# The forget floor ahead of the query copy on ScalarE, and the exponents of the head two on at the end of the step on VectorE

## The chip, the cores and the metric

The kernel runs on one core of one Trainium2 chip. The metric is the device time of one execution in microseconds; the median of several runs stands for a kernel. Five engines work in the core, each through its own list of instructions in order, and they wait for each other on semaphores: TensorE (PE: matmuls; PEld: its weight loads), VectorE (DVE), ScalarE (ACT), GpSimd (POOL) and SyncE (SP), which issues most of the transfers.

## What is computed

Two blocks of a model, one after the other, on 512 tokens of width 1024 in float32. The first block has a layer with attention and a layer with a gated recurrence; the second has a long convolution, windowed attention, pooling and a mixture of 16 experts. The change lies in the recurrence, of which this is what matters:

```python
def hgrn2_mixer(u, w_in, lb, out_gain, w_out):
    proj = u @ w_in
    q, fl, inp, g = jnp.split(proj, ...)
    log_f = jnp.logaddexp(jnp.log(lbf), jnp.log1p(-lbf) + jax.nn.log_sigmoid(fl))
    k = -jnp.expm1(log_f)
    def step(state, xs):                      # per chunk of tokens, 8 heads
        qb, kb, gb, ib = xs
        b = jnp.cumsum(gb, axis=-2)
        diff = b[..., :, None, :] - b[..., None, :, :]
        decay = jnp.exp(jnp.where(causal[:, :, None], diff, -jnp.inf))
        scores = jnp.einsum('bhtd,bhsd,bhtsd->bhts', qb, kb, decay)
        o = scores @ ib + jnp.einsum('bhtd,bhdv->bhtv', qb * jnp.exp(b), state)
        b_last = b[..., -1:, :]
        state = jnp.exp(b_last[..., 0, :])[..., None] * state + \
            jnp.einsum('bhsd,bhsv->bhdv', kb * jnp.exp(b_last - b), ib)
        return state, o
    _, o = lax.scan(step, state0, (qc, kc, gc, ic))
    o = o * lax.rsqrt(jnp.mean(o * o, axis=-1, keepdims=True) + EPS) * out_gain
    return (o * jax.nn.silu(gh)).reshape(B, S, REC_VWIDTH) @ w_out
```

## The kernel before

Each engine's list is written out by hand, and nothing reorders it. The recurrence goes head by head, h = 0 to 7, on tiles of 128 channels by 512 tokens; a head's 512 tokens are four chunks of 128. The decays between two tokens are split over seven levels (block sizes 1 to 64): for a level the exponents are differences to the middle of each block, so that they never overflow. One step h does this:

- TensorE (loop at L972): "diag" (L977), seven "level" jobs (L987), "kw" (L993, transposes of kd1), "t1" of head h - 1 (L966), the q projection of head h + 2 (L827), the three "state" jobs (L1011), the output "o1" (L1015 and L1019), and the forget projection of head h + 3 (L827). In heads 6 and 7 a small matmul for the filter of the second block stands there too (L1001, L1005), and gate projections take the place of the q and forget projections.
- VectorE (loop at L2000): forget_in(h + 2) (L1852, L1854), exponents(h + 1) (L1881 and L1882, 14 subtractions of 128 x 256), head_scores(h) (L1898 for "diag", then seven predicated copies L1910), head_turned(h - 1) (L1946), forget_log(h + 2) (L1859, L1861, L1862), head_states(h) (L1918, L1921), chunk_exponents(h + 1) (L1890), head_mean_square(h) (L1926), forget_sum(h + 2) (L1867 and the scan L1868), head_normed(h) (L1932 to L1940).
- ScalarE (loop at L1510): level_exps(h + 1) (L1473, one instruction over 3584 columns), the copy of "kw" (L1370), forget_softplus(h + 2) (L1457, L1459), the query copy of head h + 2 (L1370), forget_floor(h + 2) (L1464 to L1469), head_squares(h) (L1492), chunk_exps(h + 1) (L1480 to L1484).
- GpSimd (loop at L733): decayed_levels(h + 1), 14 products (L721, L723), after the level exponentials of h + 1 and once TensorE has read level 6 of head h; the power for the root (L738) after the mean square; decayed_chunk(h + 1), two products (L728, L729).

What ties them: forget_log waits for the softplus, the floor for forget_log, forget_sum for the floor, the exponents for the sum of their head; the mean square waits for the squares, the squares for "o1". The exponents of a head are kept in one of two buffers and may be written once TensorE has read level 6 of the head two before.

The results of TensorE go to eight PSUM banks, which a ledger (class Ledger) gives to the jobs in turn. A job that reuses a bank waits until the reader of the job eight before has emptied it. A step has 16 jobs: "diag", seven levels, "kw", "t1", the q projection, three states, "o1", the forget projection. So "kw" waits for the reader of "diag" of the same step (L1898), level 5 for the reader of "o1" of the step before (L1937), and level 6 for the reader of the forget projection before it (L1852).

Of the kernel before, what the change touches and what calls it, by code (L numbers as in the profile page):

```python
# [29 lines left out]
RH = 8  # L30
# [107 lines left out]
def before_state(h):  # L138

    return [("q1", h + 2)] if h + 2 < RH else [("g1", 3 if h == RH - 2 else 5)]  # L140


def after_output(h):

    if h + 3 < RH:
        return [("f1", h + 3)]
    return {RH - 3: [("g1", 2)], RH - 2: [("g1", 4)], RH - 1: [("g1", 6), ("g1", 7)]}[h]
# [163 lines left out]
def two_blocks(nc, a, out):  # L311

    ctx = ExitStack()
    with ctx:
# [1026 lines left out]
        def _(act):  # L1341
# [25 lines left out]
            def copy(dst, name, src=None, scale=1.0, func=ACT.Identity):  # L1367
                act.wait_ge(filled, nth(name))
                bank = led.bank(name)
                act.activation(dst, bank[:, :] if src is None else src(bank), func, scale=scale).then_inc(by_act, 1)  # L1370
# [83 lines left out]
            def forget_softplus(h):  # L1454
                w = fwork[h % 2]
                act.wait_ge(f_dve, 4 * h + 1)
                act.activation(w[1], w[1], ACT.Exp).then_inc(f_act, 1)  # L1457
                act.wait_ge(f_act, 6 * h + 1)
                act.activation(w[1], w[1], ACT.Ln, bias=1.0).then_inc(f_act, 1)  # L1459

            def forget_floor(h):
                w = fwork[h % 2]
                act.wait_ge(f_dve, 4 * h + 3)
                act.activation(w[4], w[2], ACT.Abs, bias=lw[0][:, h:h + 1]).then_inc(f_act, 1)  # L1464
                act.activation(k1[h % 2], w[3], ACT.Exp, bias=lw[3][:, h:h + 1]).then_inc(f_act, 1)
                act.wait_ge(f_act, 6 * h + 3)
                act.activation(w[4], w[4], ACT.Exp, scale=-1.0).then_inc(f_act, 1)
                act.wait_ge(f_act, 6 * h + 5)
                act.activation(w[4], w[4], ACT.Ln, bias=1.0).then_inc(f_act, 1)  # L1469

            def level_exps(h):
                act.wait_ge(expo_in, h + 1)
                act.activation(expo[h % 2], expo[h % 2], ACT.Exp).then_inc(expo_done, 1)  # L1473
# [21 lines left out]
            def late_gate(h):  # L1495
                if h >= 3:
                    act.wait_ge(head_gated, h - 2)
                copy(gate1, ("g1", h), func=ACT.Silu)
# [11 lines left out]
            for h in range(RH):  # L1510
                if h + 1 < RH:
                    level_exps(h + 1)
                copy(kw1[:, :, :], ("kw", h), src=lambda b: b[:, 0:384].rearrange("p (c t) -> p c t", c=3))
                if h + 2 < RH:
                    forget_softplus(h + 2)
                else:
                    act.wait_ge(sin_in, h - RH + 3)
                    act.activation((sine_1, sine_2)[h - RH + 2], sine_x, ACT.Sin).then_inc(sin_out, 1)
                for tag, j in before_state(h):
                    if tag == "q1":  # L1520
                        copy(q1[j % 2], ("q1", j))
                    else:
                        late_gate(j)
                if h + 2 < RH:
                    forget_floor(h + 2)
                head_squares(h)
                if h + 1 < RH:
                    chunk_exps(h + 1)
                for tag, j in after_output(h):
                    if tag == "g1":  # L1530
                        late_gate(j)
# [96 lines left out]
        def _(dve):  # L1628
# [177 lines left out]
            for m in range(KT + 1):  # L1806
                if m >= 1:
                    for n in range(2):
                        h = 2 * m - 2 + n
# [13 lines left out]
                if m < KT:  # L1823
                    for n in range(2):
                        h = 2 * m + n
# [38 lines left out]
            def forget_sum(h):  # L1864
                w = fwork[h % 2]
                dve.wait_ge(f_act, 6 * h + 6)
                step(dve.tensor_tensor(w[5], w[5], w[4], ALU.add))  # L1867
                dve.tensor_tensor_scan(b1[h % 2], reset, w[5], 0.0, ALU.mult, ALU.add).then_inc(f_dve, 1)  # L1868
                dve.wait_ge(f_dve, 4 * h + 4)

            def exponents(h):

                e = expo[h % 2]
                if h >= 2:
                    dve.wait_ge(filled, nth(("level", h - 2, LEVELS - 1)))
                for level in range(LEVELS):
                    half = 1 << level
                    ev = e[:, level, :].rearrange("p (n g s) -> p n g s", g=2, s=half)
                    bv = b1[h % 2].rearrange("p (n g s) -> p n g s", g=2, s=half)
                    mid = bv[:, :, 0, half - 1:half].broadcast_to([P, T // (2 * half), half])  # L1880
                    dve.tensor_tensor(ev[:, :, 1, :], bv[:, :, 1, :], mid, ALU.subtract)  # L1881
                    ins = dve.tensor_tensor(ev[:, :, 0, :], mid, bv[:, :, 0, :], ALU.subtract)  # L1882
                ins.then_inc(expo_in, 1)
# [40 lines left out]
            def head_mean_square(h):  # L1924
                dve.wait_ge(o_sq, h + 1)
                dve.tensor_scalar(mean[:, 0:4], ss[:, 0:4], 1.0 / P, EPS, ALU.mult, ALU.add).then_inc(head_mean, 1)  # L1926
                dve.wait_ge(head_mean, h + 1)
# [23 lines left out]
            def late_gate(h):  # L1951
                dst = mixT[1][:, h, :]
                dve.wait_ge(*drained(("t1", h)))
                dve.wait_ge(*drained(("g1", h)))
                dve.tensor_tensor(dst, dst, gate1, ALU.mult).then_inc(head_gated, 1)
# [44 lines left out]
            for h in range(RH):  # L2000
                if h + 2 < RH:
                    forget_in(h + 2)
                if h + 1 < RH:
                    exponents(h + 1)
                head_scores(h)
                if h >= 1:
                    head_turned(h - 1, mixT[1][:, h - 1, :] if h <= 2 else None)
                if h == RH - 2:
                    sine_argument(("fh1",), 0)
                elif h == RH - 1:  # L2010
                    sine_argument(("fh2",), 1)
                    sum_filter_weights()
                if h + 2 < RH:
                    forget_log(h + 2)
                head_states(h)
                if h + 1 < RH:
                    chunk_exponents(h + 1)
                if h == RH - 2:
                    late_gate(3)
                head_mean_square(h)  # L2020
                if h + 2 < RH:
                    forget_sum(h + 2)
                elif h == RH - 1:
                    late_gate(5)
                head_normed(h)
                for tag, j in after_output(h):
                    if tag == "g1" and j < RH - 1:
                        late_gate(j)
# [73 lines left out]
            for m in range(1, NH // 2 + 1):  # L2102
                for n in range(2):
                    h = 2 * m - 2 + n
# [208 lines left out]
```

## Time and profile before

| | |
|---|---|
| median of 3 runs | 2184.64 us (2183.11 to 2184.93) |
| profiled execution | 2189.95 us, its span 2188.2 us |
| busy: PE, PEld, DVE, ACT, POOL | 2043.8, 981.8, 597.4, 421.5, 198.5 us |
| mean granted clock of TensorE | 0.967 of full speed |
| recurrence | from about 515 to 795 us of the span |

The rows further down come from four views. The waits name, for an instruction that found its engine idle, who released it. The timeline gives instructions of one engine in order of time, merged where a line repeats, and in brackets the idle time just before. A view of stretches gives the busy time of every engine in a given piece of the span and PEclk, the clock granted to TensorE as a share of 2.4 GHz (0.50 is 1.2 GHz). The view of one line or tensor gives the spread of durations. Times count from the start of the span.

### The profile page before, as it was taken

How to read it: one execution, taken by the hardware profiler on the slowest of the kernel's cores; microseconds unless marked ns; L12 is line 12 of the kernel's file. 1: busy time of each engine (PE TensorE's matmuls, PEld its weight loads, DVE VectorE, ACT ScalarE, POOL GpSimd, SP SyncE). 2: the span in 40 equal slices, each digit the busy share in tenths (PEclk: the TensorE clock that was granted, in tenths of full speed). 3: DMA queues.
4: the chain of work that ended last, by engine and by line, in shares of the span. 5: the costliest groups of instructions: out<-in, count | busy, mean ns of one | idle time of the engine just before them, and what ended most of it. 6: DMA issues, size and time to landing. Idle time of an engine off the chain costs nothing.

```text
span 2188.2 us, 20253 instructions
## 1 busy us (share of the span) xinstructions
PE 2043.8 (93%) x8224; PEld 981.8 (45%) x8224; DVE 597.4 (27%) x1316; ACT 421.5 (19%) x818; POOL 198.5 (9%) x260
## 2 busy tenths in 40 slices
PE   8999999999988999999999698999989898989896
PEld 3455454444565554454655443434343332434333
DVE  2233342312677632314443410101010101101012
ACT  1233331114554511110230000000101010000002
POOL 3100000001545500000110000000000000000000
PEclk9999999999999899999999799999999999999998
DMA  7211012202111141240240599999999999999995
GB/s 262 80 58 58 1 56 89 77 10 77 39 39 39 43 183 36 75 141 0 77 156 37 211 413 429 427 428 427 428 428 427 428 428 427 428 428 427 428 427 220
DMA packets 87644, 486.36 MB, mean 222 GB/s; under 512 B 5663, under 2 KB 37754, under 8 KB 63488
## 3 DMA queue, kind: packets, MB, share of 16 engines
q1 hardware_dynamic: 84896, 480.79, 54.1%
q0 software_dynamic: 2368, 4.16, 0.7%
q8 instruction: 66, 1.08, 0.2%
q14 instruction: 26, 0.21, 0.0%
q10 hardware_dynamic: 288, 0.11, 0.0%
HBM read 482.90 MB, written 2.34 MB: 222 GB/s over the span
## 4 chain that ended last, share of the span: by engine, by line
PE 80%; DMA 12%; DVE 5%; ACT 2%; issue 1%; POOL 0%; POOLq 0%; ACTq 0%; DVEq 0%
PE bank L827 19%; PE bank L835 17%; PE bank L1284 13%; DMA arena<-in_w_up 12%; PE bank L1315 10%; PE bank L1235 3%; PE bank L1153 3%; PE bank L1261 2%; PE bank L907 2%; PE bank L1305 1%; PE bank L1039 1%; PE bank L817 1%; PE bank L1108 1%; PE bank L925 1%; PE bank L915 1%
## 5 line engine op out<-in xcount | busy, mean ns | idle before, releaser
L1284 PE MATMUL bank<-arena 128*64 128x512 f32 x2048 | 467.7, 615 | 69.8 <-DMA arena<-in_w_up 69.8
L827 PE MATMUL bank<-arena 128*128 128x512 f32 x1024 | 457.2, 606 | 0.0
L835 PE MATMUL bank<-arena 128*128 128x512 f32 x832 | 363.0, 596 | 5.1 <-issue 4.3
L1284 PEld LDWEIGHTS bank<-arena 128*64 128x64 f32 x2048 | 160.9, 142 | 373.7 <-issue 373.5
L827 PEld LDWEIGHTS bank<-arena 128*128 128x128 f32 x1024 | 196.9, 195 | 245.1 <-issue 244.7
L835 PEld LDWEIGHTS bank<-arena 128*128 128x128 f32 x832 | 157.9, 191 | 199.6 <-issue 198.4
L1315 PE MATMUL bank<-arena 128*64 128x512 f32 x960 | 217.2, 612 | 0.0
L1370 ACT ACTIVATE arena<-bank 128x512 f32<-128x512 f32 (+3 forms) x140 | 76.5, 551 | 536.8 <-PE bank L835 197.4
L2228 DVE TENSOR_TENSOR arena<-arena,bank 128x512 f32<-128x512 f32 x64 | 42.0, 685 | 410.5 <-PE bank L1261 409.8
L1587 ACT ACTIVATE arena<-bank 64x512 f32<-64x512 f32 x64 | 37.7, 589 | 553.3 <-PE bank L1284 510.9
L2243 DVE TENSOR_TENSOR arena<-bank,arena 64x512 f32<-64x512 f32 x64 | 44.4, 695 | 362.6 <-ACT arena L1587 360.7
L1315 PEld LDWEIGHTS bank<-arena 128*64 128x64 f32 x960 | 69.4, 141 | 135.7 <-issue 134.6
L801 POOL TENSOR_TENSOR small<-small 128x4 f32<-128x4 f32 x1 | 1.0, 1013 | 964.4 <-DVE small L2260 964.4
L1235 PEld LDWEIGHTS bank<-arena 128*128 128x128 f32 x512 | 62.8, 201 | 7.8 <-issue 7.8
L1235 PE MATMUL bank<-arena 128*128 128x128 f32 x512 | 64.5, 288 | 1.2 <-DVE arena L2200 1.2
L1604 ACT ACTIVATE arena<-bank,small 64x512 f32<-64x512 f32 x30 | 20.5, 682 | 211.1 <-PE bank L1315 210.9
L1153 PE MATMUL bank<-arena 128*128 128x512 f32 x128 | 58.3, 610 | 1.6 <-DVE arena L2134 1.6
L1261 PE MATMUL bank<-arena 128*128 128x512 f32 x128 | 57.3, 599 | 2.2 <-ACT arena L1612 2.2
L721 POOL TENSOR_TENSOR arena<-arena 128x256 f32<-128x256 f32 x56 | 48.2, 860 | 97.6 <-ACT arena L1473 84.9
L1389 ACT ACTIVATE arena<-arena,small 128x128 f32<-128x128 f32 (+3 forms) x96 | 49.9, 521 | 24.1 <-DVE small L1703 23.4
L987 PE MATMUL bank<-arena 128*128 128x64 f32 x448 | 50.9, 274 | 0.0
L987 PEld LDWEIGHTS bank<-arena 128*128 128x128 f32 x448 | 50.7, 192 | 0.0
(289 smaller groups left out, 1598.9 us busy)
## 6 DMA issues: line engine op xcount, KB each, us to landing
arena<-in_w_gate SPq DMA_DIRECT2D x64, 2048.0 KB, 24.6
arena<-in_w_up SPq DMA_DIRECT2D x64, 2048.0 KB, 28.5
arena<-in_w_down SPq DMA_DIRECT2D x60, 2048.0 KB, 23.9
arena<-in_att_w_in SPq DMA_DIRECT2D x12, 1024.0 KB, 11.3
arena<-in_rec_w_in SPq DMA_DIRECT2D x12, 1024.0 KB, 5.8
arena<-in_ple_w_gate SPq DMA_DIRECT2D x4, 2048.0 KB, 14.4
arena<-in_w_down SPq DMA_DIRECT2D x8, 1024.0 KB, 18.1
arena<-in_w_in SPq DMA_DIRECT2D x6, 1024.0 KB, 7.8
```

The lines of the kernel that those rows point to most:

```text
L721: pool.tensor_tensor(ev[:, :, 1, :], ev[:, :, 1, :], qv[:, :, 1, :], ALU.mult).then_inc(decayed, 1)
L827: mm = pe.matmul(bank[:, :], w[:, k, c:c + P], xT[:, k, :], start=(k == 0), stop=(k == KT - 1))
L835: mm = pe.matmul(bank[:, 0:n], xT[:, k, P * i:P * i + P], w[:, k, c:c + n], start=(k == 0), stop=(k == kt - 1))
L987: mm = pe.matmul(bank[:, 64 * c:64 * c + 64], kl1[:, level, P * c:P * c + P], ev[:, n * c:n * c + n, 1, :], start=True, stop=True)
L1153: mm = pe.matmul(bank[:, :], mixT2[:, k, P * i:P * i + P], w[:, k, :], start=(k == ks[0]), stop=(k == ks[-1]))
L1235: mm = pe.matmul(bank[:, P * k:P * k + P], hn[:, i, 256 * kq + odd:256 * kq + 256:2], ohp[:, i, :], start=(i == 0), stop=(i == TT - 1))
L1261: pe.matmul(bank[:, :], ohT[:, P * i:P * i + P], yrow[:, 512 * half:512 * half + 512], start=True, stop=True).then_inc(moe_filled, 1)
L1284: mm = pe.matmul(banks[f][64 * part:64 * part + 64, :], xe[:, k, CAP * (e % 2):CAP * (e % 2) + CAP], w[:, kk, 512 * f:512 * f + 512], star ...
L1315: mm = pe.matmul(bank[64 * half:64 * half + 64, :], hT[:, 4 * b + j, :], wd[:, j, 512 * half:512 * half + 512], start=(b == 0 and j == 0), ...
L1370: act.activation(dst, bank[:, :] if src is None else src(bank), func, scale=scale).then_inc(by_act, 1)
L1389: act.activation(s, s, ACT.Exp, bias=nmx[:, r:r + 1], accum_out=rs[:, r:r + 1]).then_inc(probs_in, 1)
L2243: dve.tensor_tensor(hrow[64:P, f, :], banks[f][64:P, :], sil[f % 2][64:P, :], ALU.mult).then_inc(h_ready2, 1)
```

## The change

On ScalarE, forget_floor(h + 2) goes ahead of the copy that follows the q projection. On VectorE, exponents(1) stays at the start of step 0; the exponents of every later head are written at the end of the step two before it, behind the mean square and ahead of head_normed. For that forget_sum(h + 2) goes ahead of head_mean_square(h).

```diff
@@ scalar, for h in range(RH) @@
                     act.activation((sine_1, sine_2)[h - RH + 2], sine_x, ACT.Sin).then_inc(sin_out, 1)
+                if h + 2 < RH:
+                    forget_floor(h + 2)
                 for tag, j in before_state(h):
                     if tag == "q1":
                         copy(q1[j % 2], ("q1", j))
                     else:
                         late_gate(j)
-                if h + 2 < RH:
-                    forget_floor(h + 2)
                 head_squares(h)
@@ vector, for h in range(RH) @@
                 if h + 2 < RH:
                     forget_in(h + 2)
-                if h + 1 < RH:
-                    exponents(h + 1)
+                if h == 0:
+                    exponents(1)
                 head_scores(h)
@@ vector, the end of the same loop @@
                 if h == RH - 2:
                     late_gate(3)
+                if h + 2 < RH:
+                    forget_sum(h + 2)
                 head_mean_square(h)
                 if h + 2 < RH:
-                    forget_sum(h + 2)
+                    exponents(h + 2)
                 elif h == RH - 1:
                     late_gate(5)
                 head_normed(h)
```

VectorE at the end of a step, first piece: from forget_sum (L1867, L1868) on; the lines with a minus are head_normed and, of the next step, forget_in.

```order
 L1867 TENSOR_TENSOR arena<-arena 128x512
 L1868 SCALAR_TENSOR_TENSOR arena<-tab,arena 128x512
-L1932 TENSOR_TENSOR small<-small 128x4
-L1933 TENSOR_TENSOR small<-small 128x4
-L1934 TENSOR_SCALAR small<-small 128x4
-L1935 TENSOR_TENSOR small<-small 128x4
-L1937 TENSOR_TENSOR arena<-bank,small 128x512
-L1940 COPY small<-small 128x1
-L1852 COPY arena<-bank 128x512
-L1854 SCALAR_TENSOR_TENSOR arena<-arena 128x512
+L1926 TENSOR_SCALAR small<-small 128x4
 L1881 TENSOR_TENSOR arena<-arena 128x256
```

The mean square L1926 now follows the sum, and the exponents (L1881, L1882, fourteen in all) follow it directly.

Second piece, 14 exponents further on, up to L1898, the first instruction of head_scores:

```order
 L1882 TENSOR_TENSOR arena<-arena 128x4x64
+L1932 TENSOR_TENSOR small<-small 128x4
+L1933 TENSOR_TENSOR small<-small 128x4
+L1934 TENSOR_SCALAR small<-small 128x4
+L1935 TENSOR_TENSOR small<-small 128x4
+L1937 TENSOR_TENSOR arena<-bank,small 128x512
+L1940 COPY small<-small 128x1
+L1852 COPY arena<-bank 128x512
+L1854 SCALAR_TENSOR_TENSOR arena<-arena 128x512
 L1898 TENSOR_TENSOR arena<-bank,tab 128x512
```

head_normed and forget_in stand behind the exponents now, directly ahead of L1898.

ScalarE in step 0, before: the end of the softplus (L1459), the query copy (L1370), the floor (L1464 to L1469), the squares (L1492).

```order
L1459 ACTIVATE arena<-arena 128x512
L1370 ACTIVATE arena<-bank 128x512
L1464 ACTIVATE arena<-arena,small 128x512
L1465 ACT_TABLE_LOAD
L1465 ACTIVATE arena<-arena,small 128x512
L1467 ACTIVATE arena<-arena 128x512
L1469 ACT_TABLE_LOAD
L1469 ACTIVATE arena<-arena 128x512
L1492 ACTIVATE arena,small<-bank 128x128 x4
```

The same place with the change:

```order
L1459 ACTIVATE arena<-arena 128x512
L1464 ACTIVATE arena<-arena,small 128x512
L1465 ACT_TABLE_LOAD
L1465 ACTIVATE arena<-arena,small 128x512
L1467 ACTIVATE arena<-arena 128x512
L1469 ACT_TABLE_LOAD
L1469 ACTIVATE arena<-arena 128x512
L1370 ACTIVATE arena<-bank 128x512
L1492 ACTIVATE arena,small<-bank 128x128 x4
```

The query copy moved from ahead of the floor to between the floor and the squares.

## Rows read from the trace of the kernel before

**Rows 1.** TensorE's waits, whole kernel: line, releaser, total us, times, longest.
```profile
PE bank L993 <- DVE arena L1898: 18.0, 6, 3.1
```

**Rows 2.** Stretches: busy us of PE, PEld, DVE, ACT, POOL, then PEclk, DMA, GB/s.
```profile
560.00:580.00 20.00, 20.00 (x112) 14.21 (x111) 9.56 (x15) 13.64 (x15) 11.48 (x14) 1.00 0.00 1
595.00:596.00 1.00, 1.00 (x3) 0.50 (x2) 0.93 (x3) 1.00 (x2) 0.00 (x0) 0.50 0.00 0
880.00:900.00 20.00, 19.16 (x57) 9.04 (x56) 10.09 (x24) 2.83 (x5) 0.54 (x1) 1.00 0.25 78
```

**Rows 3.** TensorE's timeline: start, duration, line, operation, [idle before]; three places.
```profile
574.09 0.83 PE L1011 MATMUL bank<-arena 128*128 128x128 f32 x6
...
576.32 7.03 PE L827 MATMUL bank<-arena 128*128 128x512 f32 x16
583.19 1.05 PE L977 MATMUL bank<-arena 128*128 128x128 f32 x8
...
593.56 0.52 PE L993 MATMUL bank<-tab,arena 128*128 128x128 f32 x3 [3.11 <-DVE arena L1898]
...
595.18 8.38 PE L827 MATMUL bank<-arena 128*128 128x512 f32 x16
...
753.13 0.83 PE L1011 MATMUL bank<-arena 128*128 128x128 f32 x6
...
769.32 0.50 PE L993 MATMUL bank<-tab,arena 128*128 128x128 f32 x3
...
770.19 1.07 PE L1005 MATMUL bank<-arena,fw 64*64 64x512 f32 x2
```

**Rows 4.** Timeline of VectorE: end of step h = 2 and the next.
```profile
640.36 0.17 DVE L1926 TENSOR_SCALAR small<-small 128x4 f32<-128x4 f32 x1 [4.68 <-ACT arena L1492]
640.57 0.69 DVE L1867 TENSOR_TENSOR arena<-arena 128x512 f32<-128x512 f32 x1
641.29 1.23 DVE L1868 TENSOR_TENSOR_SCAN arena<-tab,arena 128x512 f32<-128x512 f32 x1
...
642.95 1.27 DVE L1934 TENSOR_SCALAR small<-small 128x4 f32<-128x4 f32 x1
644.25 0.91 DVE L1935 TENSOR_TENSOR small<-small 128x4 f32<-128x4 f32 x1
...
647.33 0.42 DVE L1881 TENSOR_TENSOR arena<-arena 128x256 f32<-128x256 f32 x1
...
652.03 0.68 DVE L1898 TENSOR_TENSOR arena<-bank,tab 128x512 f32<-128x512 f32 x1
652.75 3.90 DVE L1910 COPY_PREDICATED arena<-maskt,bank 128x256 f32<-128x256 int32 x7
656.55 0.74 DVE L1946 TENSOR_SCALAR arena<-bank,cols 128x512 f32<-128x512 f32 x1
...
659.30 1.10 DVE L1861 TENSOR_TENSOR arena<-arena 128x512 f32<-128x512 f32 x1
```

**Rows 5.** Timeline of ScalarE, h = 3: query copy, first of floor, first square.
```profile
662.26 0.60 ACT L1370 ACTIVATE arena<-bank 128x512 f32<-128x512 f32 x1 [4.08 <-PE bank L827]
662.75 0.71 ACT L1464 ACTIVATE arena<-arena,small 128x512 f32<-128x512 f32 x1
...
667.87 0.26 ACT L1492 ACTIVATE arena<-bank 128x128 f32<-128x128 f32 x1
```

**Rows 6.** GpSimd: three rows of its timeline; durations ns (min/median/max) of L721.
```profile
640.68 1.45 POOL L738 TENSOR_TENSOR small<-small 128x4 f32<-128x4 f32 x1 [3.72 <-DVE small L1926]
642.93 1.27 POOL L728 TENSOR_TENSOR arena<-arena 128x512 f32<-128x512 f32 x1 [0.80 <-ACT arena L1484]
644.15 0.99 POOL L729 TENSOR_TENSOR arena<-arena 128x384 f32<-128x384 f32 x1
...
L721 POOL TENSOR_TENSOR arena<-arena x56: 714/838/1183, 539.9 to 753.4; 128x256 f32<-128x256 f32 x56
```

**Rows 7.** Issues of the experts' gate weights: durations, first and last start.
```profile
L630 SPq DMA_DIRECT2D arena<-in_w_gate x64: 327/328/581, 1114.7 to 2112.2; - x64
```

## The prediction

> **What bounds the kernel now.** I read the waits of TensorE first, then the granted clock in short windows, then the timelines of the four compute engines through one step of the recurrence. In the recurrence TensorE is busy but for 18.0 us, in six pieces of up to 3.1 us, at L993 on VectorE's L1898 [rows 1]. L993 is the transposes of kd1 (job "kw") in heads 1 to 6. The ledger gives jobs eight banks in turn, and a head has 16 jobs, so "kw" of a head takes the bank of "diag" of the same head, which L1898 (first instruction of head_scores) empties. L1898 comes late because the 14 subtractions of exponents(h + 1) stand ahead of it in VectorE's order: 647.33 to 652.03, L1898 directly behind at 652.03 [rows 4].
>
> The idle time is not its whole price. A stretch of one microsecond after such a gap shows a granted clock of 0.50 (1.2 GHz), while the step in which TensorE never waits shows 1.00 [rows 2]. The projection after the gap then takes 8.38 us where the same 16 matmuls took 7.03 [rows 3].
>
> **A period without the wait.** I measure a period from the start of the state matmuls (L1011) to the next. The six from 574.09 to 753.13 (heads 1 to 6) take 179.04, 29.84 on average [rows 3]. At full clock and with no wait a period would be:
> - 574.09 to the moment at which "kw" could have started, 593.56 less its idle 3.11 = 590.45: 16.36 us;
> - "kw" and the transposes of "t1": 769.32 to 770.19 in head 7, where nothing waits: 0.87;
> - the q projection, as long as the forget projection with its 16 matmuls, 576.32 to 583.19: 6.87.
> Together 24.10 us. Inside it, counted from its start: forget projection at 2.2, "diag" at 9.1, seven level groups of 0.91 (an eighth of 583.19 to 590.45) from 10.0, so level 5 at 14.6 and level 6 at 15.5, "kw" at 16.4. The sixth period has one filter matmul more (1.07) [rows 3].
>
> **The change on ScalarE.** The forget floor (L1464 to L1469, 662.75 to 667.87 = 5.12 us) now goes ahead of the query copy, which waited for the q projection until 662.26. Its input is L1861, done at 660.40 [rows 4, 5]. So the floor starts some 2.3 us earlier. Behind it now wait the query copy (0.49 until L1464) and the squares of o1. The copy's readers are far: GpSimd multiplies with that query a head later, and its bank is wanted by level 1 at 10.9 of the period, the copy ending near 3.6. The squares end near 4.7 instead of 6.9. Nothing is added here, so the cost is nothing, as long as the floor ends before about 10 of the period.
>
> **The change on VectorE.** The same instructions run; the sum of forget h + 2 goes ahead of the mean square, and 14 subtractions (4.70 us) move from in front of L1898 of the next head to in front of head_normed of this one. Moving them alone would leave L1898 where it was, since both places lie ahead of it; the gain is that VectorE is not idle before them (L1926, the mean square, let it stand 4.68 us for the squares, with the sum queued behind it [rows 4]) and that TensorE no longer runs slow. What is late next? I follow the loop through VectorE and ScalarE that no longer passes through TensorE:
> - floor 5.12 [rows 5];
> - sum, 640.57 to 642.52: 1.95 [rows 4]; mean square 0.17, say 0.2 [rows 4];
> - exponents 4.70 [rows 4];
> - what GpSimd takes from VectorE. L1934 and L1935, four columns each, took 1.27 and 0.91 beside L728 and L729 of 1.27 and 0.99 at the same moments [rows 4, 6]. Without company such an instruction takes 0.17 (L1926), so these two multiplications cost VectorE 1.10 + 0.75 = 1.85. They will now meet the exponents, which also read two SBUF operands: I charge 1.85 there;
> - head_normed and forget_in: 642.52 to 647.33 less that same 1.85: 2.96 [rows 4];
> - L1898 0.72, the seven predicated copies to 656.55 3.80, L1946 0.65, the two steps of forget_log 2.2 (L1861 1.10) [rows 4].
> Sum 24.15, with three handovers between the engines of some 0.05 each (an estimate) 24.3 us. TensorE's own period is 24.10. So the two are nearly equal, and VectorE's loop sets the pace by a little. In the period the exponents then run from about 5.3 to 11.9, L1937 is done by 13.4 (its bank is wanted by level 5 at 14.6), L1852 by 14.2 (level 6 at 15.5), L1898 by 15.5 ("kw" at 16.4). Three waits that could take the place of the old one each have about 1 us to spare. ScalarE's level exponentials and GpSimd's level products come earlier too; GpSimd starts once level 6 has been read, 16.4, and needs 14 products of 0.84 in the median, 11.7 us [rows 6], until 3.8 of the next period, ahead of "diag" at 9.1.
>
> The bounds of the contention: below, none (VectorE in the shadow of TensorE, 24.10). Above, the exponents lose all the time of the three GpSimd operations beside them, 1.45 for the power and 2.26 for the two products, 3.7 [rows 6]: the loop is then 26.15. I take 1.85, the row of the same two GpSimd operations.
>
> Here a rule of the Trainium skill speaks against the change ("SBUF — State Buffer", the summary of rules for kernel authors): a VectorE instruction with two SBUF inputs and a GpSimd instruction that reads SBUF shut each other out, and the second to issue waits for the whole of the first. This trace agrees: L1861 took 1.10 beside a product of GpSimd where L1867, equally large, took 0.69 alone [rows 4]. By that rule taken for every exponent the loss would be that of the rival on the slower side, below.
>
> **The sum.** Six periods of 24.3 and the filter matmul's 1.07: 146.9, against 179.04: 32.1 us less. Of this about 18 is the idle time of [rows 1] and 14 the time lost at 1.2 GHz and while it is regained. Behind the recurrence everything hangs on TensorE's progress: the first expert slab is issued at 1114.7 behind a TensorE job, and the stream of slabs then runs without a break [rows 7]. So I pass all of it on, less 0.1 for small waits in heads 6 and 7: 32.0. The profiled execution, 2189.95 us with a span of 2188.2, would become 2158 with a span of 2156. The median of the runs is 2184.64, 5.3 below the profiled one; less 32.0 it is 2152.6.
>
> **Rivals.**
> 1. *A new, shorter wait.* If GpSimd costs the exponents more than 2.8 (1.85 and the spare microsecond), level 5 waits for L1937. At the bound of 3.7 a period is 26.2, the six with the filter matmul 158.3: 20.7 less, 2163.9. Between: 2156 to 2164. For it speaks that all three margins are near 1 us; against it that no row shows more than 1.85 lost to these operations. Chance 0.25.
> 2. *The clock does not come back.* The level groups are short matmuls, and if these keep the clock low, only the 18.0 of idle time goes: 2166.6. Against it: head 0, with the same groups and no gap, ran at 1.00, and so did a stretch with 0.84 us of idle time [rows 2]. Chance 0.04.
> 3. *The gain is lost behind the recurrence,* or TensorE waits as before since something else was late together with L1898: no change. Nothing in the waits shows a second releaser there. Chance 0.04.
> 4. *Slower.* Each of the 14 exponents is shut out by GpSimd, as L1861 was: 14 x 0.41 = 5.7 in place of 1.85. Then the loop is 28.2, TensorE stands about 4 us at level 5, and it comes out of the gap at 1.2 GHz for the levels, "kw" and the projection; with the 2.6 us that a period loses to that now, near 30.8 against 29.84: 6 us slower, 2190. It decides when the exponents take over 10 us instead of 4.7. Against it: GpSimd has only 3.7 us of work there. Chance 0.03.
>
> **The numbers.** My case, a period of 24.1 to 24.6 (2151 to 2155), has 0.64; the likeliest time is 2152.6. The range 2149 to 2165 takes in no contention at all (33.4 less: 2151), a little for the clock elsewhere, and the whole of rival 1. What a measurement can tell from no change is about 0.2% (4.4 us). Faster by more than that: cases 0, 1 and 2, 0.93. Within: rival 3, 0.04. Slower: rival 4, 0.03.
>
> **What would show it.** Right: L993's wait on L1898 gone or below 0.5 us, granted clock 1.00 from 560 to 750, periods of 24.1 to 24.6 us, L1934 and L1935 at 0.17, the exponents at 6 to 7 us for 14 with L728 and L729 beside them, the floor starting within 0.1 us of L1861's end. Wrong: a wait of TensorE at L987 on L1937 (rival 1; over 2 us rival 4), clock below 1.00 without gaps (rival 2), a saved recurrence but the first expert slab not 32 us earlier (rival 3).

## The result, and the profile after

| | before | changed |
|---|---|---|
| median (runs) | 2184.25 us (4) | 2153.68 us (4), 2150.02 to 2158.01 |
| ratio | | 0.9861, 95% interval 0.9842 to 0.9880 |
| profiled execution, its span | 2189.95, 2188.2 us | 2150.02, 2148.2 us |
| six periods of the recurrence, heads 1 to 6 | 179.04 us | 148.40 us |

The change is worth 30.6 us; 32.0 had been forecast (2152.6, counted from a median of 2184.64). A second set of runs gave 2153.00 beside 2184.18, ratio 0.9845 (0.9829 to 0.9861).

The 18.0 us of [rows 1] are gone. These are the waits of TensorE in the changed kernel from 540 to 780 us (line, releaser, us in total, times, longest): the one at L993 is down to 0.2 us, once.

```profile
PE bank L966 <- DVE arena L1910: 0.7, 3, 0.3
PE bank L827 <- DVE arena L1910: 0.7, 4, 0.2
PE bank L987 <- DVE arena L1937: 0.3, 1, 0.3
PE bank L993 <- DVE arena L1898: 0.2, 1, 0.2
```

The timeline of TensorE, for comparison with [rows 3]: the first two periods, 567.74 to 593.29 and to 617.39, and the end of the sixth. In the first, small waits at four places; in the second, none from "kw" (609.48) to the next period, and the projection behind it takes 7.11 us where 8.38 stood.

```profile
567.74 0.83 PE L1011 MATMUL bank<-arena 128*128 128x128 f32 x6
...
582.62 1.97 PE L987 MATMUL bank<-arena 128*128 128x64 f32 x16 [0.32 <-DVE arena L1937]
584.75 0.52 PE L993 MATMUL bank<-tab,arena 128*128 128x128 f32 x3 [0.16 <-DVE arena L1898]
585.55 0.63 PE L966 MATMUL bank<-tab,arena 128*128 128x128 f32 x4 [0.28 <-DVE arena L1910]
586.35 7.10 PE L827 MATMUL bank<-arena 128*128 128x512 f32 x16 [0.17 <-DVE arena L1910]
593.29 0.83 PE L1011 MATMUL bank<-arena 128*128 128x128 f32 x6
...
609.48 0.50 PE L993 MATMUL bank<-tab,arena 128*128 128x128 f32 x3
...
610.44 7.11 PE L827 MATMUL bank<-arena 128*128 128x512 f32 x16
617.39 0.83 PE L1011 MATMUL bank<-arena 128*128 128x128 f32 x6
...
716.14 0.83 PE L1011 MATMUL bank<-arena 128*128 128x128 f32 x6
```

A stretch of the changed kernel, as in [rows 2]. TensorE is busy in nearly all of 600 to 620, at a granted clock of 1.00 (2.4 GHz); the whole stretch from 560 to 750 shows 1.00 too.

```profile
600.00:620.00 20.00, 19.97 (x114) 14.31 (x114) 17.71 (x34) 10.88 (x11) 12.66 (x15) 1.00 0.00 1
```

VectorE at the end of step 0, the place of [rows 4] one period after the other: the mean square, then the fourteen exponents, two of them at 1.48 and 1.21 us where the others take 0.41, then head_normed with L1934 at 0.17 instead of 1.27, and L1898.

```profile
574.21 0.17 DVE L1926 TENSOR_SCALAR small<-small 128x4 f32<-128x4 f32 x1
574.42 0.43 DVE L1881 TENSOR_TENSOR arena<-arena 128x256 f32<-128x256 f32 x1
...
576.11 1.48 DVE L1882 TENSOR_TENSOR arena<-arena 128x256 f32<-128x256 f32 x1
577.51 1.21 DVE L1881 TENSOR_TENSOR arena<-arena 128x256 f32<-128x256 f32 x1
...
581.38 0.17 DVE L1934 TENSOR_SCALAR small<-small 128x4 f32<-128x4 f32 x1
...
581.78 0.69 DVE L1937 TENSOR_TENSOR arena<-bank,small 128x512 f32<-128x512 f32 x1
...
583.92 0.68 DVE L1898 TENSOR_TENSOR arena<-bank,tab 128x512 f32<-128x512 f32 x1
```

What stands beside the two slow ones is on GpSimd, at the same moments:

```profile
575.85 1.46 POOL L728 TENSOR_TENSOR arena<-arena 128x512 f32<-128x512 f32 x1
577.27 1.17 POOL L729 TENSOR_TENSOR arena<-arena 128x384 f32<-128x384 f32 x1
```

And the floor on ScalarE no longer stands behind the query copy as in [rows 5]; it waits for VectorE's L1861, which ended at 591.08:

```profile
591.11 0.72 ACT L1464 ACTIVATE arena<-arena,small 128x512 f32<-128x512 f32 x1 [2.85 <-DVE arena L1861]
```

**The two profiled executions differ by more than the change.** Their spans are 40.0 us apart, the medians 30.6. The first state matmuls already start 6.35 us earlier (574.09 and 567.74), in code that the change does not touch. The stretch from 50 to 150 us shows why, first the kernel before, then the changed one: the granted clock was 0.95 there in one execution and 1.00 in the other.

```profile
50.00:150.00 100.00, 98.25 (x260) 44.50 (x259) 25.70 (x75) 24.42 (x53) 13.02 (x24) 0.95 0.24 75
```

```profile
50.00:150.00 100.00, 98.25 (x281) 45.25 (x280) 26.92 (x77) 24.90 (x55) 11.75 (x22) 1.00 0.25 79
```

In a second profiled execution of the changed kernel the same stretch was at 0.95 and the first state matmuls started at 573.78, yet its six periods took 148.41 us. All twelve profiled executions fall on one side or the other: at 0.95 in this stretch the first state matmuls start at 573.2 to 574.1 (four of them), at 1.00 at 567.1 to 568.4 (eight). So this is chance from one execution to the next. Of the 40.0 us, 6.35 lie ahead of the recurrence, 30.6 in its six periods and some 3 further back. I read the experiments by the sum of the six periods (from the first start of L1011's group to the seventh), with the medians beside it. The two kernels that were profiled twice gave the same sum to 0.01 us; both ran at full clock in every period. The kernel before and the other experiments have one trace each, and where the clock falls in some periods the sum may repeat less well.

### The profile page after: what moved, and what is told of

Same layout as the page of the kernel before. It is cut to its first block, busy times and chain, and to the rows that moved or that the text cites. A ratio compares the mean times of both kernels' runs of the same rounds, so it can differ in the third digit from the quotient of the medians.

```text
span 2148.2 us, 20253 instructions
## 1 busy us (share of the span) xinstructions
PE 2023.5 (94%) x8224; PEld 971.8 (45%) x8224; DVE 598.5 (28%) x1316; ACT 421.7 (20%) x818; POOL 199.3 (9%) x260
## 4 chain that ended last, share of the span: by engine, by line
PE 81%; DMA 12%; DVE 4%; ACT 1%; issue 1%; POOL 0%; POOLq 0%; ACTq 0%; DVEq 0%
PE bank L827 19%; PE bank L835 17%; PE bank L1284 13%; DMA arena<-in_w_up 12%; PE bank L1315 10%; PE bank L1235 3%; PE bank L1153 3%; PE bank L1261 2%; PE bank L907 2%; PE bank L1305 1%; PE bank L987 1%; PE bank L1039 1%; PE bank L817 1%; PE bank L1108 1%; PE bank L925 1%
## 5 line engine op out<-in xcount | busy, mean ns | idle before, releaser
L827 PE MATMUL bank<-arena 128*128 128x512 f32 x1024 | 446.1, 594 | 0.7 <-DVE arena L1910 0.7
L835 PE MATMUL bank<-arena 128*128 128x512 f32 x832 | 362.0, 595 | 5.1 <-issue 4.2
L827 PEld LDWEIGHTS bank<-arena 128*128 128x128 f32 x1024 | 192.4, 190 | 238.0 <-issue 237.9
L835 PEld LDWEIGHTS bank<-arena 128*128 128x128 f32 x832 | 157.6, 191 | 198.9 <-issue 197.7
L1370 ACT ACTIVATE arena<-bank 128x512 f32<-128x512 f32 (+3 forms) x140 | 76.4, 550 | 512.4 <-PE bank L835 196.5
L1235 PEld LDWEIGHTS bank<-arena 128*128 128x128 f32 x512 | 62.3, 200 | 7.8 <-issue 7.8
L1261 PE MATMUL bank<-arena 128*128 128x512 f32 x128 | 57.3, 600 | 2.2 <-ACT arena L1612 2.2
L1153 PE MATMUL bank<-arena 128*128 128x512 f32 x128 | 56.7, 595 | 1.6 <-DVE arena L2136 1.6
L721 POOL TENSOR_TENSOR arena<-arena 128x256 f32<-128x256 f32 x56 | 48.3, 862 | 75.9 <-PE bank L987 51.1
L987 PE MATMUL bank<-arena 128*128 128x64 f32 x448 | 51.1, 274 | 0.3 <-DVE arena L1937 0.3
L987 PEld LDWEIGHTS bank<-arena 128*128 128x128 f32 x448 | 50.7, 192 | 0.4 <-issue 0.4
```

The lines of the kernel that those rows point to most:

```text
L721: pool.tensor_tensor(ev[:, :, 1, :], ev[:, :, 1, :], qv[:, :, 1, :], ALU.mult).then_inc(decayed, 1)
L827: mm = pe.matmul(bank[:, :], w[:, k, c:c + P], xT[:, k, :], start=(k == 0), stop=(k == KT - 1))
L835: mm = pe.matmul(bank[:, 0:n], xT[:, k, P * i:P * i + P], w[:, k, c:c + n], start=(k == 0), stop=(k == kt - 1))
L987: mm = pe.matmul(bank[:, 64 * c:64 * c + 64], kl1[:, level, P * c:P * c + P], ev[:, n * c:n * c + n, 1, :], start=True, stop=True)
L1153: mm = pe.matmul(bank[:, :], mixT2[:, k, P * i:P * i + P], w[:, k, :], start=(k == ks[0]), stop=(k == ks[-1]))
L1235: mm = pe.matmul(bank[:, P * k:P * k + P], hn[:, i, 256 * kq + odd:256 * kq + 256:2], ohp[:, i, :], start=(i == 0), stop=(i == TT - 1))
```

## Experiments

| kernel | six periods, us | one by one | median, us | ratio to before (95%) |
|---|---|---|---|---|
| before | 179.04 | 29.30 30.01 28.66 29.69 30.20 31.18 | 2184.2 to 2185.5 | 1 |
| changed | 148.40 | 25.55 24.10 24.81 24.34 24.58 25.02 | 2153.68 | 0.9861 (0.9842 to 0.9880) |
| changed, again | 148.41 | 25.54 24.11 24.83 24.31 24.59 25.03 | 2153.00 | 0.9845 (0.9829 to 0.9861) |
| ScalarE's edit alone | 161.24 | 27.42 27.07 27.07 25.51 28.54 25.63 | 2167.46 | 0.9913 (0.9897 to 0.9929) |
| VectorE's edit alone | 169.28 | 27.64 27.47 27.42 27.42 27.42 31.91 | 2175.03 | 0.9944 (0.9930 to 0.9959) |
| before, gap filled with 12 matmuls | 175.26 | 29.01 five times, 30.21 | 2185.00 | 0.9986 (0.9973 to 0.9998) |
| before, gap filled with 6 matmuls | 168.03 | 27.96 27.96 27.95 27.97 27.95 28.24 | 2178.03 | 0.9958 (0.9942 to 0.9973) |
| changed, GpSimd's products held back | 145.21 | 24.48 23.83 23.86 24.07 23.83 25.14 | 2152.19 | 0.9840 (0.9820 to 0.9861) |
| the same, again | 145.21 | 24.48 23.83 23.86 24.06 23.83 25.15 | 2154.85 | 0.9848 (0.9828 to 0.9869) |
| changed, four exponents more | 155.50 | 27.45 25.42 25.59 25.58 25.60 25.86 | 2160.72 | 0.9895 (0.9880 to 0.9910) |
| changed, mean square first | 155.65 | 27.05 25.01 25.66 26.99 24.62 26.32 | 2160.49 | 0.9899 (0.9883 to 0.9915) |
| changed, head_normed first | 157.98 | 28.61 24.57 27.19 25.21 26.58 25.82 | 2164.03 | 0.9900 (0.9885 to 0.9916) |

The sixth period of each has the filter matmul.

### Each edit alone

ScalarE's edit alone:

```diff
+                if h + 2 < RH:
+                    forget_floor(h + 2)
                 for tag, j in before_state(h):
...
-                if h + 2 < RH:
-                    forget_floor(h + 2)
```

> The kernel before with the edit on ScalarE alone (the forget floor of head h + 2 ahead of the query copy); VectorE as before. Theory (the loop through VectorE and ScalarE sets the pace, and the exponents stand ahead of L1898): the floor no longer waits for the q projection, so the loop is shorter by about 2 us a head, but the mean square still holds back the sum. TensorE still waits at L993, 0.5 to 2.6 us instead of 3.1, perhaps by turns, and the clock falls less often: 10 to 20 us faster than before (2165 to 2174). Rival (the edit on ScalarE only makes room, the gain is VectorE's): within 4 us of before, L993 still at 3.1 us a head.

It was 18.1 us faster by the medians and 17.8 by the periods. TensorE's waits there, from 540 to 780:

```profile
PE bank L993 <- DVE arena L1898: 6.4, 5, 2.0
```

The gap at L993 fell from 18.0 to 6.4 us without one instruction of VectorE moved. What held L1898 back was the start of the floor as much as the place of the exponents, and the rival falls. The waits are shorter, but the clock still fell behind four of them, the shortest 0.89 us, in head 3:

```profile
640.14 0.52 PE L993 MATMUL bank<-tab,arena 128*128 128x128 f32 x3 [0.89 <-DVE arena L1898]
```

```profile
641.00:642.00 1.00, 1.00 (x5) 0.91 (x6) 0.96 (x2) 1.00 (x1) 0.00 (x0) 0.50 0.00 0
```

VectorE's edit alone:

```diff
-                if h + 1 < RH:
-                    exponents(h + 1)
+                if h == 0:
+                    exponents(1)
...
+                if h + 2 < RH:
+                    forget_sum(h + 2)
                 head_mean_square(h)
                 if h + 2 < RH:
-                    forget_sum(h + 2)
+                    exponents(h + 2)
```

> The kernel before with the edit on VectorE alone (sum ahead of the mean square, exponents of head h + 2 behind it); ScalarE as before. Theory: the floor waits for the q projection again, 2.3 us later, and so do the sum and everything behind it; TensorE waits 1 to 2 us at level 5 on L1937 and under 0.5 us at L993, periods near 26.3 us: 12 to 20 us faster than before (2164 to 2172), less if the clock falls. Rival (the edit on VectorE is the whole gain): 30 us faster, as the two together, 2154.

It was 10.5 us faster by the medians (9.8 by the periods), less than the 12 to 20 expected, and far from the 30 of the rival, which falls. The wait did move to level 5 on L1937, 1.76 us in every head (10.6 in all). The forecast had named the clock ("less if the clock falls") and given it no price; it fell behind the wait in every head: five periods are 27.42 to 27.64 where 26.3 was expected, and the sixth is 31.91. That one, head 6, is the worst: "kw", "t1", the filter matmul (1.97) and the projection, 9.50 us where 7.03 is full speed, all run slow:

```profile
721.75 2.92 PE L987 MATMUL bank<-arena 128*128 128x64 f32 x16 [1.76 <-DVE arena L1937]
724.46 0.85 PE L993 MATMUL bank<-tab,arena 128*128 128x128 f32 x3
...
726.10 1.97 PE L1001 MATMUL bank<-arena,fw 33*64 33x512 f32 x2
727.99 9.50 PE L827 MATMUL bank<-arena 128*128 128x512 f32 x16
```

One-microsecond stretches of the same kernel give the granted clock: 1.00 in the gap, 0.50 in each of those from 723 to 732. (In head 1 it is 0.50 or near it only from 586 to 589.)

```profile
724.00:725.00 1.00, 1.00 (x7) 1.00 (x7) 0.96 (x2) 0.00 (x0) 0.15 (x1) 0.50 0.00 0
...
730.00:731.00 1.00, 1.00 (x3) 0.48 (x2) 0.97 (x2) 0.00 (x0) 1.00 (x2) 0.50 0.00 0
```

The two edits alone give 17.8 and 9.8 us, 27.6 in sum, and together 30.6. TensorE's busy and idle time over the six periods tells where the 3 us are. Idle time goes down by 10.5 and 7.9 us alone and by 16.6 together; busy time, of the same instructions, by 7.3 and 1.9 alone and by 14.0 together. Most of the 3 us is the slow clock, then, which only both edits remove (its granted mean over the six periods is 0.90 before, 0.96 and 0.92 with one edit, 1.00 with both).

### The clock's share

To separate idle time from the slow clock behind it, TensorE was kept at work in the gap of the kernel before, writing columns of the level 6 bank that nobody reads. (The filler is work that the reference does not ask for; nothing of the computation is left out.)

```diff
                 for level in range(LEVELS):
...
+                    if level == LEVELS - 1 and 1 <= h <= RH - 2:
+                        for _ in range(12):
+                            pe.matmul(bank[:, 256:512], ident, i1[:, 0, 0:256], start=True, stop=True)
```

> The kernel before, and in heads 1 to 6 TensorE runs 12 more matmuls of 128x256 ahead of level 6, into columns of its bank that nobody reads. They fill about 2.7 of the 3.1 us in which TensorE was idle; no wait of another engine ends sooner, so the only thing that can change is the clock. Theory (14 of the 32 us are lost to the clock after the gap): granted clock 1.00 through the recurrence, the q projection after the gap at 7.0 instead of 8.4 us, 9 to 15 us faster than before (2169 to 2175). Rival (the time after the gap is not the clock's, or VectorE's loop takes it back since it never waited for TensorE): within 3 us of before.

The six periods are 3.8 us shorter and the median 0.5 (ratio 0.9986), not the 9 to 15 expected; what the clock is worth cannot be read from that, since the filler was too long. The timeline shows 24 instructions and 5.40 us for the 12 matmuls, so that TensorE itself, without a wait and at a clock of 1.00, set a period of 29.01:

```profile
611.46 5.40 PE L988 MATMUL bank<-arena,tab 128*128 128x256 f32 x24
```

With range(6) in place of range(12):

> The kernel before with half the filler: 6 matmuls of 128x256 ahead of level 6 in heads 1 to 6 (the first try with 12 showed 24 instructions and 5.2 us, 2.1 more than the gap, so TensorE itself set a period of 29.01 and the comparison told nothing of the clock's price). Now the filler takes 2.6 of the 3.1 us. Theory: the clock stays at 1.00; the loop before ran from the end of the q projection to L993 (19.47 us) and then through L993, L966 and the next q projection, which are 7.7 us at full clock: a period of 27.2 instead of 29.84, 13 to 16 us faster than before, 2169 to 2172, with a rest of idle time of 0.3 to 0.6 us a head. Rival (what follows the gap is slow for another reason, or the loop does not pass through the projection): periods stay near 29, within 4 us of before.

Periods of 27.96, 11.0 us less over the six, against the 13 to 16 expected; the medians say 6.7, and the interval of the ratio 5.9 to 12.7. Here is one period of it: the filler takes 2.81 us, a rest of 0.52 us remains at L996 (which is L993 shifted by the edit), and the projection behind it is at full speed.

```profile
595.60 0.83 PE L1014 MATMUL bank<-arena 128*128 128x128 f32 x6
...
610.90 2.81 PE L988 MATMUL bank<-arena,tab 128*128 128x256 f32 x12
...
615.07 0.52 PE L996 MATMUL bank<-tab,arena 128*128 128x128 f32 x3 [0.52 <-DVE arena L1901]
615.84 0.63 PE L966 MATMUL bank<-tab,arena 128*128 128x128 f32 x4 [0.26 <-DVE arena L1913]
616.62 7.11 PE L827 MATMUL bank<-arena 128*128 128x512 f32 x16 [0.15 <-DVE arena L1913]
623.56 0.83 PE L1014 MATMUL bank<-arena 128*128 128x128 f32 x6
```

The time from the start of the period to "kw" is 19.47 us, to the hundredth what it was in [rows 3] (574.09 to 593.56): no other engine was late or early by itself. The rest is 8.49 us where I had expected 7.7. Of this "t1" and the projection wait 0.26 and 0.15 us for the predicated copies that follow L1898; their starts are some 0.3 us later still, in the same places, and the view does not show that as idle time. That the time came down at all needs the loop to pass through TensorE: in the kernel before, the floor waited for the copy of the projection, so a faster projection made every later step earlier.

The 11.0 us are what the clock gives back while VectorE's and ScalarE's orders stay as they were. They are not yet its share of the 30.6. For that, here are the six periods of the kernel before, the changed one and the half-filled one; behind the length of the stretch stands TensorE's busy time:

```profile
574.09:753.13 179.04, 160.56 (x742) 104.13 (x740) 128.68 (x248) 93.25 (x146) 95.07 (x109) 0.90 0.12 37
```

```profile
567.74:716.14 148.40, 146.53 (x741) 97.58 (x740) 129.22 (x248) 92.08 (x144) 94.12 (x107) 1.00 0.14 45
```

```profile
567.64:735.67 168.03, 163.02 (x814) 111.40 (x813) 127.24 (x248) 92.59 (x145) 92.13 (x105) 1.00 0.13 40
```

Before, TensorE was idle for 18.5 us, after the change for 1.9, and the same work took 160.6 and 146.5 us busy. So the 30.6 are 16.6 of idle time and 14.0 of busy time, and the granted clock went from 0.90 to 1.00. Busy time is not the clock's to the last microsecond: the kernel with GpSimd's products held back (below) also ran at 1.00 and has 144.7, so I take the 14.0 to be slow clock within some 2 us (an estimate from these rows). The half-filled kernel agrees: 163.0 less six fillers of 2.81 is 146.2, so there the slow clock is gone as well. About 3 us of it came back as waits, for filler and idle time together are 21.9 us where 18.5 were idle.

### What sets the pace now

> The changed kernel with four of the fourteen exponents of heads 2 to 7 written twice (the same values, after a semaphore of VectorE's own): about 1.4 us more on VectorE between the mean square and head_normed. Theory (VectorE's loop sets the pace now, by a little): periods longer by 1.2 to 1.4 us, waits of TensorE at level 5 of about 1 us, 7 to 9 us slower than the changed kernel, 2161 to 2163, if the clock holds. Rival (TensorE sets the pace and VectorE has a microsecond to spare): at most 3 us slower.

```diff
-                for level in range(LEVELS):
+                levels = list(range(LEVELS)) + ([LEVELS - 2, LEVELS - 1] if h >= 2 else [])
+                for at, level in enumerate(levels):
+                    if at == LEVELS:
+                        step(ins)
```

The periods grew by 7.1 us, the median by 7.0 (2160.7, just under the 2161 to 2163 expected). VectorE had nothing to spare: 1.4 us more a head cost 1.2. The first period alone grew by 1.9: its wait at level 5 was 1.8 us, and the clock fell to 0.50 behind it. In the others that wait was 0.2 to 0.4 us, less than the 1 us expected, and the clock stayed at 1.00 from 589 on. TensorE's waits, from 540 to 780, stand where the forecast put the next late thing, at level 5 on head_normed (L1940 here is L1937 shifted), and the copies and L1898 behind it follow:

```profile
PE bank L987 <- DVE arena L1940: 3.5, 6, 1.8
PE bank L966 <- DVE arena L1913: 1.1, 4, 0.3
PE bank L993 <- DVE arena L1901: 0.6, 4, 0.2
```

The other side, GpSimd's two products moved away from the exponents:

```diff
+                if h + 3 < RH:
+                    pool.wait_ge(f_dve, 4 * h + 13)
                 if h + 1 < RH:
                     decayed_chunk(h + 1)
```

> The changed kernel, with one wait more on GpSimd: its two products L728 and L729 begin only when VectorE has finished forget_in of head h + 3 (heads 0 to 4), so that they stand beside L1898 and the predicated copies, which read PSUM, and not beside the exponents. Theory (the two products take 1.85 us from the exponents, and VectorE's loop is just above TensorE's 24.1): all 14 exponents at 0.42, none at 1.2 to 1.5, VectorE 1.8 us a head earlier at L1898, TensorE without any wait in heads 1 to 6, periods 24.1; 1 to 3 us faster than the changed kernel (2151 to 2153), hardly more than the measurement tells. Rival (the slow exponents are slow by themselves, by their strides): the two slow ones stay, periods as in the changed kernel.

Its GpSimd waits for VectorE's L1856 (L1854 shifted, the end of forget_in), and VectorE's exponents of that head, 598.32 to 603.02, ran at 0.41 to 0.43 each, none slower; the pair that was slow in the changed kernel is regular here, so the strides are not the cause.

```profile
606.17 1.27 POOL L728 TENSOR_TENSOR arena<-arena 128x512 f32<-128x512 f32 x1 [6.55 <-DVE arena L1856]
```

```profile
598.32 0.43 DVE L1883 TENSOR_TENSOR arena<-arena 128x256 f32<-128x256 f32 x1
...
603.02 0.15 DVE L1934 TENSOR_TENSOR small<-small 128x4 f32<-128x4 f32 x1
```

TensorE's only wait from 540 to 780 is 0.4 us, in the first head, for the product that is now held back itself:

```profile
PE bank L995 <- POOL arena L729: 0.4, 1, 0.4
```

The periods are 3.2 us shorter in sum, slightly more than the 1 to 3 expected, and the median 1.5. The shortest fall to 23.83, which is then TensorE's own. I had computed 24.10. Both kernels were timed again, side by side:

> The changed kernel once more, beside chunk_late_again on the same chip, since the two were not timed in one call before. Expected 2151 to 2157; the six periods of the recurrence at 148 to 149 us in its profile, as in its first profile (148.4), whatever the rest of the execution does.

> The changed kernel with GpSimd's two products held back until VectorE has finished forget_in. By the six periods of its first profile (145.2 against 148.4) it should be 3 us faster than the changed kernel on the same chip; rival: the 3 us are within what one execution differs from the next, and the medians show nothing.

Both sums came back within a hundredth, 148.41 and 145.21. In the medians, 2153.00 and 2154.85, the 3.2 us are not to be seen: single runs of either kernel lie 7.5 to 8.7 us apart, more than the difference. By the trace this is the best version; by the clock on the wall it cannot be told from the changed kernel.

### The order at the end of the step

```diff
+                head_mean_square(h)
                 if h + 2 < RH:
                     forget_sum(h + 2)
-                head_mean_square(h)
```

> The changed kernel with head_mean_square back ahead of forget_sum; the exponents stay behind both. Theory: the sum then waits for the squares, which end 1.5 us after the floor, so sum and exponents start 1.6 us later in a loop that has nothing to spare: 7 to 10 us slower than the changed kernel, 2161 to 2164. Rival (once the floor is early the order of the two is indifferent): within 2 us of the changed kernel.

7.3 us more in the periods, 6.8 by the medians: the sum must stand ahead of the mean square, since the squares end later than the floor. Of the 7.3, 3.3 are idle time and 3.9 busy time, most of it the clock's (0.98 in the mean). The periods are uneven (27.05, 25.01, ..., 26.99), because the clock fell in some heads and not in others. In head 1 it fell behind a wait of 1.37 us:

```profile
583.28 2.48 PE L987 MATMUL bank<-arena 128*128 128x64 f32 x16 [1.37 <-DVE arena L1937]
```

In head 4 it fell behind waits of 0.44, 0.16 and 0.27 us (L987, L993, L966), and the projection took 8.40 us; one head earlier, waits of 0.45, 0.16 and 0.27 at the same lines left it at 1.00, and the projection took 7.11. The length of the waits alone does not tell whether the clock falls.

```profile
634.42 1.97 PE L987 MATMUL bank<-arena 128*128 128x64 f32 x16 [0.45 <-DVE arena L1937]
...
638.12 7.11 PE L827 MATMUL bank<-arena 128*128 128x512 f32 x16 [0.15 <-DVE arena L1910]
...
660.08 1.97 PE L987 MATMUL bank<-arena 128*128 128x64 f32 x16 [0.44 <-DVE arena L1937]
...
663.83 8.40 PE L827 MATMUL bank<-arena 128*128 128x512 f32 x16
```

And head_normed ahead of the exponents:

```diff
                 head_mean_square(h)
                 if h + 2 < RH:
+                    head_normed(h)
                     exponents(h + 2)
```

> The changed kernel with head_normed ahead of the exponents (after sum and mean square). The bank of o1 is then emptied 5 us earlier, so level 5 has room, but VectorE stands 1.2 to 1.5 us for GpSimd's power in each head. Theory (what counts is VectorE's whole loop, not the one bank): 5 to 9 us slower than the changed kernel, 2159 to 2163, TensorE waiting at L993 on L1898 again, 0.5 to 1.5 us. Rival (the bank of o1 at level 5 is what limits the changed kernel): same or faster than the changed kernel.

9.6 us more in the periods, 10.4 by the medians, slightly past the 5 to 9 expected. VectorE does stand idle for the power as expected, 1.26 us in head 1, but TensorE waits elsewhere: at level 6 on L1852, and at L993 only 0.5 us in all. These waits cost 3.0 us of idle time more than in the changed kernel; the other 6.6 are busy time, mostly because the clock fell to 0.50 in or soon behind each of the three waits at level 6 (1.44, 0.79 and 0.77 us), a price that the forecast did not have.

```profile
PE bank L987 <- DVE arena L1852: 3.0, 3, 1.4
PE bank L993 <- DVE arena L1898: 0.5, 2, 0.3
```

L1852 is the next instruction of VectorE whose bank is wanted once L1937 is early; moving one reader ahead only uncovers the next.

## Why the prediction was right, point by point

- **What bounds.** Right: TensorE, held at L993 by L1898, and slowed behind the gap. The six periods came down by 30.6 us, against 32.1 in the sum. Their mean without the filter matmul is 24.56, inside the 24.1 to 24.6 that was named as the sign, near its upper end.
- **TensorE's own period.** 24.10 was computed, 23.83 is what it takes when nothing waits (kernel with the products held back). Of the 0.27, 0.17 lies in the moment at which "kw" could start: I had taken it as 593.56 less the idle time, 16.36 us into the period; in a head without a wait "kw" starts at 609.48 - 593.29 = 16.19. Idle time counts from the modelled end of the last matmul, and the rows show that the next one starts a little before it. The other 0.10 lies in "kw" and "t1", 0.87 in head 7 and 0.77 where nothing waits. That the second period of the changed kernel is 24.10 to the hundredth is luck: behind "kw" it takes 7.91 us against 7.64 in the kernel with the products held back, though the view shows no wait there. The error did no harm, since VectorE's loop was the longer one.
- **VectorE's loop.** 24.3 was computed; from one L1926 to the next it took 24.13 (574.21 to 598.34), and a mean of 24.4 over the next five. The terms held to within 0.25 us (forget_log took 1.95 here and 2.2 a head later, for 2.2). The floor started 0.03 us behind L1861, the exponents with their contention took 6.57 us (574.42 to 580.99) for 4.70 + 1.85 = 6.55.
- **The contention.** The charge of 1.85 was the least sure term and came out at (1.48 - 0.42) + (1.21 - 0.41) = 1.86. The same two products of GpSimd cost VectorE the same time in both places. The prediction says of L1934 and L1935 that they too read two SBUF operands; L1934 reads one tensor with two constants, and was held up all the same (1.27 for 0.17). Held back behind forget_in, the products cost VectorE nothing: L1898 took 0.68 beside them.
- **The mis-sized term** is the first period: 25.55, where all six had been put at 24.3 (the last with the filter matmul's 1.07 on top). In head 0 forget_log waited 2.80 us for the softplus, the floor ended 4.0 us into the period instead of 3.0, and the sum (L1867) met a product of GpSimd and took 1.15 instead of 0.69. That is 1.25 of the 1.5 us by which the sum was off. The other 0.46 of this kind returns in every second head or so (L1867 at 1.14 in the third), which makes the 24.8 among the 24.1.
- **The split of the gain,** 18 idle and 14 clock, held: 16.6 and 14.0 by TensorE's idle and busy time. With the gap filled and nothing else changed, 11.0 of it reach the period and about 3 turn into waits.
- **That moving the exponents alone leaves L1898 where it was** missed in one point: VectorE's whole edit alone brought 9.8 us, by the sum that no longer waits for the squares. But a wait at level 5, 10.6 us in all, took the place of the 18.0 at L993 (the wait of rival 1), and the clock went on falling behind it, so that busy time came down by only 1.9 of the 14.0 us.
- **Rivals.** Rival 1 appeared as 0.32 us in one head. Rival 2 (the short matmuls of the levels keep the clock low) falls: 1.00 from 560 to 750. Rival 3 falls: the first expert slab is issued 36.9 us earlier (1114.7 and 1077.8), the 6.35 that came ahead of the recurrence and the 30.6 of it. Rival 4's size was 5.7 us of contention a head; 1.86 was there.

## What to carry to other kernels

When an engine waits for another, follow the loop from that release back to itself through all engines before moving anything: here it ran through two queues, in each of which an instruction that nobody needed yet stood ahead of one that the loop waited for, and each of the two orders was worth part of the gain. Price a regular gap on TensorE by the period and not by the idle time, since the matmuls behind it can run slow (nearly half of the 30.6 us here), and look at what is late next before counting on more than the slack of that bank or buffer. And read a difference of a few microseconds from sums over the same stretch of several traces; for the two kernels traced twice here they repeated to 0.01 us where whole executions differed by 8.

## What the runs showed of the hardware

- The granted clock of TensorE fell to 0.50 behind regular gaps much shorter than the 3.1 us of the kernel before: 1.76 us in every head (VectorE's edit alone), 0.89 with 0.26 behind it (ScalarE's edit alone), 0.77 (head_normed first). It stayed at 1.00 behind 0.66 and 0.26 in one head of ScalarE's edit alone, and behind 0.52, 0.26 and 0.15 in each period of the half-filled kernel. Between them nearly the same waits, 0.44, 0.16, 0.27 and 0.45, 0.16, 0.27, went one way and the other.
- The same stretch of the same code, 50 to 150 us, ran at 1.00 in eight executions and at 0.95 in four, and the recurrence began some 6 us later in these. The profiled executions of before and changed happened to fall on different sides.
- A VectorE instruction with two operands in SBUF lost nearly the whole length of a GpSimd product that began shortly before it: 1.48 for 0.42 beside a product of 1.46, 1.21 for 0.41 beside one of 1.17. The Trainium skill says that the second of two such instructions waits for the whole of the first ("SBUF — State Buffer", the summary of rules for kernel authors), and this trace agrees for the products. It does not for the power on 128x4 (L738, 1.22 us), which reads SBUF too and cost the exponents beside it nothing (0.42 each).
- A float32 matmul of 128x256 shows as two instructions, and 12 of them took 5.40 us.
